# Stick-breaking logits made two steps ahead, in three buffers and three PSUM banks of their own

## The reference

```python
z = einsum('bhqd,bhkd->bhqk', q, k) * dh ** -0.5      # logits
mask = kpos[None, :] < qpos[:, None]
log_beta = log_sigmoid(z)
log_rem = where(mask, log_beta - z, 0.0)              # minus softplus(z)
between = cumsum(log_rem, axis=3, reverse=True) - log_rem
w = where(mask, exp(log_beta + between), 0.0)
o = einsum('bhqk,bhkd->bhqd', w, v)
...
merged = g_a * (o_sb @ w_o_sb) + g_b * (o_hg @ w_o_hg)
h = x + merged @ w_out
h = h + square(relu(rmsnorm(h) @ w_ff1)) @ w_ff2
```

## Time and profile before

| | before |
|---|---|
| runs, us | 801.05, 798.27, 801.79 (median 801.05) |
| profiled execution: own time | 798.5 us |
| its span in the profile | 796.7 us |
| mean granted clock of PE | 0.955 |
| PE busy | 704.1 us (88%) |
| DVE busy | 355.3 us (45%) |
| ACT busy | 301.2 us (38%) |
| POOL busy | 46.5 us (6%) |
| HBM read | 208.32 MB |

### The profile page before, as it was taken

One profiled execution on the slowest core, in us unless ns is written; L12 is line 12 of the kernel. 1 busy time (PEld: TensorE's weight loads), 2 busy tenths in 40 slices (PEclk: granted clock), 3 DMA queues, 4 the chain that ended last, 5 costly groups with the idle time before them and its releaser, 6 DMA issues.

```text
span 796.7 us, 12576 instructions
## 1 busy us (share of the span) xinstructions
PE 704.1 (88%) x5226; PEld 543.5 (68%) x5226; DVE 355.3 (45%) x563; ACT 301.2 (38%) x444; POOL 46.5 (6%) x84
## 2 busy tenths in 40 slices
PE   3999889989877676668999999698998999999996
PEld 2787658853332132224999889597977999999995
DVE  2567742342010010106846883345476455554543
ACT  4344440241110010005765443477355434444342
POOL 0000000000000000000093820000000000000000
PEclk9999999999998699889999999799899999999999
DMA  8998799989999999999745343214334455544101
GB/s 340 416 415 342 261 369 424 419 352 422 423 422 422 424 421 424 418 410 421 276 158 211 138 182 107 106 32 181 102 112 172 169 211 211 186 179 172 45 1 53
DMA packets 33036, 210.24 MB, mean 264 GB/s; under 512 B 4688, under 2 KB 5072, under 8 KB 8656
## 3 DMA queue, kind: packets, MB, share of 16 engines
q1 hardware_dynamic: 32976, 209.38, 66.3%
HBM read 208.32 MB, written 1.05 MB: 263 GB/s over the span
## 4 chain that ended last, share of the span: by engine, by line
PE 67%; DMA 19%; DVE 7%; ACT 4%; issue 2%; SPq 1%; DVEq 0%; ACTq 0%
PE psum L419 66%; DMA raw<-in_w_exp 16%; DMA early<-in_w_ada_q 2%; DVE wlo L520 2%; ACT whi L495 1%; PE psum L427 1%; DVE acc L544 1%; SPq L474 0%; DVE XL L1972 0%; ACT Sp L846 0%; DVE XL L2352 0%; SPq L466 0%; DVE X L2394 0%; ACT G L1299 0%; ACT gates L1942 0%
## 5 line engine op out<-in xcount | busy, mean ns | idle before, releaser
L419 PE MATMUL psum<-XH,whi 128*128 128x256 f32 x736 | 212.3, 288 | 7.1 <-DVE XL L2352 2.9
L419 PE MATMUL psum<-XH,wlo 128*128 128x256 f32 x736 | 209.8, 285 | 0.0
L419 PE MATMUL psum<-XL,whi 128*128 128x256 f32 x736 | 209.7, 285 | 0.0
L520 DVE TENSOR_TENSOR wlo<-raw,whi 128x2048 fp32r<-128x2048 f32 (+1 forms) x88 | 168.9, 1957 | 50.3 <-ACT whi L495 50.3
L419 PEld LDWEIGHTS psum<-XH,whi 128*128 128x128 f32 x736 | 141.3, 192 | 10.7 <-DVE XL L2352 3.1
L495 ACT ACTIVATE whi<-raw 128x2048 fp32r<-128x2048 f32 (+1 forms) x79 | 139.2, 1801 | 22.6 <-PE psum L419 22.4
L419 PEld LDWEIGHTS psum<-XL,whi 128*128 128x128 f32 x736 | 140.7, 191 | 0.3
L419 PEld LDWEIGHTS psum<-XH,wlo 128*128 128x128 f32 x736 | 140.9, 191 | 0.0
L419 PE MATMUL psum<-raw,G 128*32 128x512 f32 x456 | 68.4, 686 | 19.9 <-DMA raw<-in_w_exp 19.8
L419 PEld LDWEIGHTS psum<-raw,G 128*32 128x32 f32 x456 | 17.9, 124 | 56.8 <-issue 56.1
L419 PE MATMUL psum<-raw,XT 128*32 128x512 f32 x248 | 36.4, 721 | 20.2 <-DMA raw<-in_w_exp 19.0
(11 more groups left out here) (340 smaller groups left out, 965.4 us busy)
## 6 DMA issues: line engine op xcount, KB each, us to landing
raw<-in_w_exp SPq DMA_DIRECT2D x85, 1024.0 KB, 23.6
raw<-in_w_ff SPq DMA_DIRECT2D x32, 1024.0 KB, 5.8
raw<-in_w_in SPq DMA_DIRECT2D x22, 1024.0 KB, 5.7
raw<-in_w_ada SPq DMA_DIRECT2D x16, 1024.0 KB, 10.1
raw<-in_w_in_t SPq DMA_DIRECT2D x8, 1024.0 KB, 17.6
X<-in_w_exp SPq DMA_DIRECT2D x5, 1024.0 KB, 24.6
raw<-in_w_ada_q SPq DMA_DIRECT2D x4, 1024.0 KB, 15.1
raw<-in_w_out_t SPq DMA_DIRECT2D x4, 1024.0 KB, 8.2
```

Of the source, the lines that this page charges most:

```text
L419: return e.matmul(o, l, r, start=start, stop=stop, skip_group_check=True)
L520: e.tensor_tensor(wlo[j % NS][:, x], ring[slot[i]][:, x], whi[j % NS][:, x], ALU.subtract).then_inc(*steps_(("lo", j, x.start // 1024), *[ ...
```

## The change

Heads 0 and 1 of the logits, with ACT's and DVE's work on them, are made in the loop of the recurrence heads, for head 3, right behind the first gate quarter and `values` (on ACT behind `act_head`, on DVE behind the scaling of the head). In the loop, step i then makes z(i+1) in place of z(i), for i from 1 to 6; step 0 is gone. `zt` has three buffers in place of two, the third a tensor of its own, and ACT's first write of z(h) waits for w(h-3) in place of sbv(h-2). `NON` has its own tensor and is written at the beginning of the block. The logits take banks 0, 1, 2 in turn; all else in the loop takes banks 3 to 7 in turn (`ob`), up to the first part of `o_sb`, which takes 2, 0, 1, 3 (`sb_`); after it, banks 4 to 7 (`wb`). The ring of eight, `banks` of the caller, stays at the place where head 3 left it, and the feed-forward layer's first four takes come from there. The number and shape of instructions stays as it is.

```diff
@@ -263,9 +263,9 @@
         tmpA = xn2[:, 0, :]
         tmpB = xn2[:, 1, :]
         EE = [XT, gates[:, 8:16, :]]
-        zt = [tmpA[:, 0:384], tmpA[:, 512:896]]
+        zt = [tmpA[:, 0:384], tmpA[:, 512:896], ta("zt2", [128, 384])[:, :]]
         zs = [tmpB[:, 0:384], tmpB[:, 512:896]]
-        NON = tmpA[:, 896:1024]
+        NON = ta("non", [128, 128])[:, :]
...
@@ -1840,21 +1840,14 @@
                         act_gate(e, 4 * (hd - 2), q)
                     if q == 0:
                         act_head(e, hd)
+                        if hd == 3:
+                            act_z(e, 0)
+                            act_z(e, 1)
                 act_pieces(e, 148 + 2 * hd)
-            for i in range(11):
-                if i < 8:
-                    b, p = i % 2, bank(("z", i))[:, 0:384]
-                    e.wait_ge(*at(("z", i)))
-                    if i >= 2:
-                        e.wait_ge(*at(("sbv", i - 2)))
-                    if i == 0:
-                        e.wait_ge(*at(("decays", 3)))
-                    e.activation(zt[b], p, ACT.Abs).then_inc(*hyb_act())
-                    e.wait_ge(*hyb_act.last())
-                    e.activation(zt[b], zt[b], ACT.Exp, scale=-1.0).then_inc(*hyb_act())
-                    e.wait_ge(*hyb_act.last())
-                    e.activation(zt[b], zt[b], ACT.Ln, bias=1.0).then_inc(*hyb_act(("z_log", i)))
-                if 1 <= i <= 8:
+            for i in range(1, 11):
+                if i < 7:
+                    act_z(e, i + 1)
+                if i <= 8:
                     h = i - 1
                     e.wait_ge(*at(("w_masked", h)))
...
+        def act_z(e, h):
+            z = zt[h % 3]
+            e.wait_ge(*at(("z", h)))
+            if h >= 3:
+                e.wait_ge(*at(("w", h - 3)))
+            if h == 0:
+                e.wait_ge(*at(("decays", 3)))
+            e.activation(z, bank(("z", h))[:, 0:384], ACT.Abs).then_inc(*hyb_act())
+            e.wait_ge(*hyb_act.last())
+            e.activation(z, z, ACT.Exp, scale=-1.0).then_inc(*hyb_act())
+            e.wait_ge(*hyb_act.last())
+            e.activation(z, z, ACT.Ln, bias=1.0).then_inc(*hyb_act(("z_log", h)))
...
+            e.tensor_scalar(NON, C["ones"], -1.0, None, ALU.mult).then_inc(*hyb_dve("non"))
...
@@ -2024,6 +2031,9 @@
                         *hyb_dve(*[("read", ("hv", hd)), ("on", hd)] if t else []))
                 if hd < 3:
                     dve_head(e, hd + 1)
+                else:
+                    dve_z(e, 0)
+                    dve_z(e, 1)
                 dve_pieces(e, 148 + 2 * hd)
                 e.wait_ge(*at(("on_turned", hd)))
...
-            e.wait_ge(*at(("decays", 3)))
-            e.tensor_scalar(NON, C["ones"], -1.0, None, ALU.mult).then_inc(*hyb_dve("non"))
-            for i in range(11):
-                if 1 <= i <= 8:
+            for i in range(1, 11):
+                if i <= 8:
                     h = i - 1
...
-                if i < 8:
-                    z = zt[i % 2]
-                    e.wait_ge(*at(("z_log", i)))
-                    e.scalar_tensor_tensor(out=z, in0=bank(("z", i))[:, 0:384], scalar=0.0, in1=z, op0=ALU.max, op1=ALU.add).then_inc(
-                        *hyb_dve())
-                    e.wait_ge(*hyb_dve.last())
-                    d = z.rearrange("p (a b) -> p a b", a=3)[:, 0:3:2, :]
-                    e.tensor_tensor(d, d, row2(C["su"]), ALU.mult).then_inc(*hyb_dve(("z_soft", i)))
+                if i < 7:
+                    dve_z(e, i + 1)
                 dve_pieces(e, SB_PIECES[i])
...
+        def dve_z(e, h):
+            z = zt[h % 3]
+            e.wait_ge(*at(("z_log", h)))
+            e.scalar_tensor_tensor(out=z, in0=bank(("z", h))[:, 0:384], scalar=0.0, in1=z, op0=ALU.max, op1=ALU.add).then_inc(*hyb_dve())
+            e.wait_ge(*hyb_dve.last())
+            d = z.rearrange("p (a b) -> p a b", a=3)[:, 0:3:2, :]
+            e.tensor_tensor(d, d, row2(C["su"]), ALU.mult).then_inc(*hyb_dve(("z_soft", h)))
...
         def pe_hybrid(e, banks):
+
+            zb, ob, sb_, wb = Banks([0, 1, 2]), Banks([3, 4, 5, 6, 7]), Banks([2, 0, 1, 3]), Banks([4, 5, 6, 7])
...
@@ -2175,24 +2187,22 @@
                         pe_gate(e, banks, w2(14 + 2 * (hd - 2)), 4 * (hd - 2), q)
                         if q == 0:
                             values()
+                            if hd == 3:
+                                banks = ob
+                                pe_z(e, zb, 0)
+                                pe_z(e, zb, 1)
                 if hd < 3:
                     pe_head(e, banks, hd + 1)
                 p = banks.take(e, ("on", hd))
                 e.wait_ge(*at(("on", hd)))
                 turn(e, p[:, 0:128], hon[:, 0, :])
                 turn(e, p[:, 128:256], hon[:, 1, :]).then_inc(*hyb_pe(("on_turned", hd)))
...
-            for i in range(11):
-                if i < 8:
-                    r, p = slice(64 * (i % 2), 64 * (i % 2) + 64), banks.take(e, ("z", i))
-                    if i == 0:
-                        for q in range(2):
-                            e.wait_ge(*at(("sq", "out", q)))
-                            e.wait_ge(*at(("sk", "out", q)))
-                    mm(e, p[:, 0:256], sbk[r, i // 2, 0:128], sbq[r, i // 2, 0:256], True, False)
-                    mm(e, p[:, 256:384], sbk[r, i // 2, 128:256], sbq[r, i // 2, 128:256], False, False).then_inc(*hyb_pe(("z", i)))
-                if 1 <= i <= 8:
+            for i in range(1, 11):
+                if i < 7:
+                    pe_z(e, zb, i + 1)
+                if i <= 8:
                     h = i - 1
-                    p, z = bank(("z", h)), zt[h % 2]
+                    p, z = bank(("z", h)), zt[h % 3]
                     e.wait_ge(*at(("z_soft", h)))
                     e.wait_ge(*at("non"))
...
                 if i == 9:
                     for n in (0, 1):
-                        pe_narrow(e, banks, w2(24), (0, 1), n, ("o_sb", n))
+                        pe_narrow(e, sb_, w2(24), (0, 1), n, ("o_sb", n))
+                    banks = wb
                 if 2 <= i < 10:
                     h = i - 2
...
                 if i == 9:
                     for n in (2, 3):
-                        pe_narrow(e, banks, w2(24 + n // 2), (0, 1), n % 2, ("o_sb", n))
+                        pe_narrow(e, sb_, w2(24 + n // 2), (0, 1), n % 2, ("o_sb", n))
...
+        def pe_z(e, banks, h):
+            r, p = slice(64 * (h % 2), 64 * (h % 2) + 64), banks.take(e, ("z", h))
+            if h == 0:
+                for q in range(2):
+                    e.wait_ge(*at(("sq", "out", q)))
+                    e.wait_ge(*at(("sk", "out", q)))
+            mm(e, p[:, 0:256], sbk[r, h // 2, 0:128], sbq[r, h // 2, 0:256], True, False)
+            mm(e, p[:, 256:384], sbk[r, h // 2, 128:256], sbq[r, h // 2, 128:256], False, False).then_inc(*hyb_pe(("z", h)))
```

## The result

The changed kernel ran at 789.42, 790.05, 785.74 and 787.51 us, median 788.46, against 800.64 for the kernel before (four runs, 798.27 to 801.79). The ratio of the two kernels is 0.9844 (95% interval 0.9811 to 0.9877), which is 12.5 us less (9.8 to 15.1); the medians themselves lie 12.2 apart. Forecast were 787.4 (783.5 to 792) and a gain of 13.6. The profiled execution took 789.42 us with a span of 787.6, mean granted clock 0.959, PE busy 705.3 us, DVE 355.1, ACT 301.4: the work is the same as before within 1.2 us on each engine, and the waits changed.

The account below looks back on a forecast made before the run. PE was taken to bound the kernel, its loop losing 10.98 us idle and 5.1 to slow clock. Idle minus 8.5 and clock minus 5.1 make 13.6, so 801.05 - 13.6 = 787.4 us, range 783.5 to 792.

Parts of the forecast that it names:

- The first gap: PE's 7.63 us idle before w(0) at 505.74 goes; a new wait of 0.55 us comes before z(3).
- The second gap: PE's 2.88 us idle before w(6) at 555.42 is replaced by a wait of 1.4 us before sbv(5).
- The clock: Slow PE clock after the gaps before w(0) and w(6) costs 2.1 and 3.05 us; 5.1 us come back.
- a wait of 1.4 us is too short for the clock to fall: Before sbv(5): assumed from two examples, 2.87 us of idling with a fall and 7.5 us with 3.3 idle without.
- The case of a gain of 10.6 us: Run whose gap before w(6) lets no clock fall come: 2.1 us of clock in place of 5.1 to regain.
- Rival A: Clock falls anyway, at the 1.4 us wait or gaps around 603.5; 3 us each, time 790.5 to 793.5; chance 0.17.
- a longer tail: Behind the loop: the prediction is wrong if the tail grows because weights now come late; unchanged length was expected.
- NON: 128x128 scaling on DVE moved to the stage's start: worth 0, and 0.13 us if PE's cover there were gone.
- Banks: Three banks for z, five for the rest in the loop, n4 turns in 0 to 3: no wait of their own, 0.
- Rival B: Five banks too few: PE stops at some 14 takes in steps 3 to 9, 4 us, time 791.5; chance 0.06.
- C: Early logits push out ACT's exponentials; z(3) to z(7) each stop PE, 805 at 3.5 us each; chance 0.03.
- D: Gap at 505.74 only moves to w_exp(0), behind 4.5 us of low parts; about 800.5; chance 0.04.

## Why the prediction was right, and where it was not

*The first gap.* Forecast: w(0) at once, a new wait of 0.55 before z(3). Measured: no gap, 0.69. Less the 4.38 us by which the profile was late at head 3, z(3) starts at 506.41, forecast was 506.4. (PE's end of the gate quarter adds up to 505.82 and not to 505.85, which changes nothing.) ACT's and DVE's early work lay in idle time as reckoned (496.68 to 499.77 on ACT; done at 500.82 on DVE). Right.

*The second gap.* Forecast 1.4 us before sbv(5) in place of 2.88 before w(6); measured 1.31, behind the block of 8.24 us that was read from the earlier trace rows. Less the same 4.38 us sbv(5) starts at 545.59, forecast was 545.6. With w_exp(5) taken before z(7) it is gone: w_exp(5) then comes 1.51 us sooner behind the block, which is the 1.5 us of z(7) on ACT. Right. The three waits of the loop make 2.47 us together, forecast 2.45.

*The clock.* Forecast 5.1 us back, from equal work at both levels; the loop ran at 1.00. Of the 13.66 us 8.51 are idle time, which leaves 5.15 for the clock. Right for this stretch in both profiles of the change. That a wait of 1.4 us is too short for the clock to fall was an assumption from two examples. It held in both profiles, but there is luck in it: with three banks for the rest the clock fell once behind waits of 1.22 and 0.37 us. The case of a gain of 10.6 us, in which the gap before w(6) lets no fall come, was met in none of the four profiles that have this gap; the mildest of the four falls is the 10.46 us in place of 11.89 above. Rival A is nonetheless real, at another place: behind the n4 turns the clock fell in seven of the nine profiles with a changed loop and its own banks, at 1.2 to 1.8 us a time where the prediction had 3, and in none of the five with the one ring. The prediction had named a longer tail as a sign against it, by late weights; the tail did grow in these seven, by the clock. The two profiles of the change had no such fall. What it takes from the average run isn't shown by these. It could account for a measured 12.5 beside a stretch of 13.66, and so could a later arrival at head 3 or the scatter, since the interval is 9.8 to 15.1.

*NON.* This step failed: "0, and 0.13 if that cover were gone". It priced only where the instruction goes, not what it frees: w(0) waited for two operands behind the same low parts, z_soft(0) and NON. The earlier trace rows named DVE L2058, the softplus, as the releaser, because DVE made it right behind NON; the wait for NON, over just before, showed in no row. At its old place the line costs 8.4 us (72.62 against 64.25). The sum was right only because the change moves it too, which as a matter of reasoning was luck.

*Banks.* "No wait of its own: 0" holds for the change, even with three banks in place of five (0.37). Rival B is out. The sentence under it that the trace before has the clock at 1.00 where PE is busy was a wrong reading: the earlier trace rows has 0.51 and 0.57 with PE busy, behind the two gaps. What the prediction did not price is the reverse: the look-ahead in the one ring loses all but 0.5 us of the gain, since a held z bank stops the ring. The banks of their own are no side matter but a condition. The n4 turns in banks 0 to 3, put at 0, cost 0.2 us.

*Rivals C and D.* ACT was nowhere a step late: the new waits are two, of 0.69 and 1.31 us. D's picture, a gap that stays, did occur, with z(0) early alone, by NON and not by w_exp(0).

*Own time.* Forecast for the profiled execution 784.9, measured 789.42; a difference of 4.5, of which 4.4 were there at 176 us already, long before the changed code. The forecast for the median was 1.1 off.

The Trainium skill, "TensorE: Matmul & The Clock Gate", Part 1, says that how many matmuls of one kernel run slowly before the clock comes up differs from run to run, with the phase of the clock gate's monitor when the kernel starts. The two profiles of the kernel with three banks agree that it differs: the same waits at the same place, once with 3.2 us at 0.51 and once at 1.00, 66.30 against 64.84. Whether a phase decides it no run shows. The Trainium skill, "TensorE: Matmul & The Clock Gate", section "A second HAM failure mode: psum-queue depth-cycling", has PE idle briefly between groups of matmuls as it cycles through banks, and the clock swing from that. No run here shows it: the kernel with three banks has one new wait, of 0.37 us, and the four waits of the one ring are few and long (1.09 to 3.77).

## What to carry to other kernels

Before moving a late operand up, list every semaphore that its consumer waits for, and look at what each stands behind. The profile shows only the last releaser of a wait, and two operands behind the same queue must both be moved (here each alone was worth nothing, the two together 10.2 us, of which 1.4 were a milder clock fall elsewhere).

Making a value earlier makes its buffer live longer. A round-robin ring of banks then stops everyone at the longest holder; give the long-lived values their own banks, count how few the others need (three cost one wait of 0.37 us), and ask the same of each buffer (the third one was worth 0.2 us).

When waits of one to three microseconds are at stake, compare a stretch between two marks of the timeline beside the whole executions: here whole runs of the changed kernel scattered by 4 us, while the stretch repeated within 0.02 in both pairs of profiles in which the clock held. Read what lies behind the stretch as well: in seven of nine profiles a part of the gain was lost there.

## What was unexpected of the hardware

Falls of PE's clock didn't follow the length of the gap. The gap of 2.88 before w(6) made it fall at its end, that of 2.85 in another kernel only behind it; behind waits of 1.22 and 0.37 close together it was at 0.51 once, and at 1.00 the next time; a gap of 2.90 left it at 1.00 in five profiles and in a sixth it was 0.66 over the next 5 us. A fall cost 1.2 to 3 us. The first matmul behind the n4 turns started 0.31 us after the last XL with the turns in banks 0 to 3, and 0.10 after it with banks 6, 7, 0, 1. The products are the same and PE's waits ahead of them are not; which makes the difference, no run tells. By the kernel's text the first product needs only the first quarter of XH and XL, while PE waits there until all turns in banks 0 to 3 were read; what a later wait would save of the 2.9 to 3.1 us was not tried.
